# Retention block of a decoder trunk: the sample queries stand in pairs, at every second sample

## What is computed

```python
    def step(s, inp):
        qc, kc, vc = inp
        a = jnp.einsum('bnhk,bmhk->bhnm', qc, kc) * decay
        o = (jnp.einsum('bhnm,bmhv->bnhv', a, vc)
             + jnp.einsum('bnhk,bhkv->bnhv', qc, s) * xi[None, :, :, None])
        s = g_c[None, :, None, None] * s + jnp.einsum('bmhk,bmhv->bhkv', kc * zeta[None, :, :, None], vc)
        return s, o
...
    o, s = retention_scan(q, k, v, s0)
    mu = jnp.mean(o, axis=-1, keepdims=True)
    var = jnp.mean(jnp.square(o - mu), axis=-1, keepdims=True)
    o = (o - mu) * lax.rsqrt(var + GN_EPS)
    o = o.reshape(B, L, hv) * jax.nn.silu(g.astype(jnp.float32))
    return o.astype(xn.dtype) @ w_out, s
```

## Time and profile before

| | |
|---|---|
| time, median of 3 runs | 1866.96 us (1866.75 to 1867.14) |
| the profiled execution | 1866.61 us, span 1864.6 us |
| PE | 1791.1 us busy, 96% of the span |
| DVE, ACT, POOL | 52%, 47%, 46% |
| chain that ended last | PE 84%, DVE 6%, ACT 3%, DMA 3%, POOL 2% |
| DMA | 346.36 MB, mean 186 GB/s |

### The profile page before, as it was taken

The page is one execution under the profiler, slowest core; times in us unless marked ns, Lnnn a source line. Parts: engine busy times, 40 slices in busy tenths (PEclk is TensorE's granted clock), DMA queues, the critical chain, the costliest instruction groups (busy, mean ns, idle before and its releaser), DMA issues.

```text
span 1864.6 us, 33101 instructions
## 1 busy us (share of the span) xinstructions
PE 1791.1 (96%) x14552; PEld 1694.6 (91%) x14552; DVE 962.8 (52%) x1035; ACT 877.5 (47%) x1020; POOL 861.3 (46%) x246
## 2 busy tenths in 40 slices
PE   8999999999979999899999988999999999999998
PEld 7888888999969999898989878999998888889998
DVE  4444446675386753334344455776354444377743
ACT  4455545443454444444454445443454555544443
POOL 4554545545215554564444402355355544555551
PEclk9999999999989999999999979999999999999999
DMA  8767864555434556755555532455667778545552
GB/s 273 243 235 274 290 216 157 181 181 165 130 106 158 178 178 201 209 178 167 154 154 166 148 90 91 141 178 162 206 199 277 242 258 283 193 140 178 180 186 86
DMA packets 306037, 346.36 MB, mean 186 GB/s; under 512 B 7847, under 2 KB 269479, under 8 KB 305887
## 3 DMA queue, kind: packets, MB, share of 16 engines
q1 hardware_dynamic: 257968, 260.36, 44.3%
q10 hardware_dynamic: 47927, 83.90, 13.0%
HBM read 299.66 MB, written 44.82 MB: 185 GB/s over the span
## 4 chain that ended last, share of the span: by engine, by line
PE 84%; DVE 6%; ACT 3%; DMA 3%; POOL 2%; issue 1%; ACTq 1%; DVEq 0%; PEldq 0%
PE acc L1481 21%; PE acc L1488 20%; PE acc L1482 20%; PE mix L1889 2%; POOL w_lo L1385 2%; PE mix L1862 1%; PE mix L1543 1%; PE acc L1509 1%; DMA st<-in_state_ret_dram 1%; PE mix L1623 1%; PE acc L1510 1%; PE acc L1515 1%; PE mix L1642 1%; ACT w_hi L434 1%; PE mix L1612 1%
## 5 line engine op out<-in xcount | busy, mean ns | idle before, releaser
L1385 POOL TENSOR_TENSOR w_lo<-raw,w_hi 128x2048 fp32r<-128x2048 f32 (+2 forms) x181 | 777.4, 4302 | 596.8 <-ACT w_hi L434 596.8
L1481 PE MATMUL acc<-g_hi,w_hi 128*128 128x264 f32 x2544 | 640.9, 290 | 9.5 <-ACT w_hi L434 3.3
L1482 PE MATMUL acc<-g_lo,w_hi 128*128 128x264 f32 x2544 | 629.7, 285 | 0.0
L434 ACT ACTIVATE w_hi<-raw 128x2048 fp32r<-128x2048 f32 (+3 forms) x260 | 455.9, 1755 | 184.1 <-PE acc L1488 87.1
L1481 PEld LDWEIGHTS acc<-g_hi,w_hi 128*128 128x128 f32 x2544 | 480.1, 189 | 22.1 <-issue 16.4
L1482 PEld LDWEIGHTS acc<-g_lo,w_hi 128*128 128x128 f32 x2544 | 482.7, 190 | 1.3
L933 DVE TENSOR_TENSOR w_lo<-raw,w_hi 128x2048 fp32r<-128x2048 f32 (+2 forms) x79 | 334.2, 4231 | 238.7 <-ACT w_hi L434 238.7
L1488 PE MATMUL acc<-g_hi,w_lo 128*128 128x264 f32 x2544 | 342.1, 285 | 0.0
L1488 PEld LDWEIGHTS acc<-g_hi,w_lo 128*128 128x128 f32 x2544 | 325.3, 188 | 2.4 <-issue 1.3
L1419 POOL TENSOR_TENSOR h_lo<-hid,h_hi 128x528 fp32r<-128x528 f32 x44 | 59.0, 1340 | 330.3 <-ACT h_hi L707 330.3
L1481 PE MATMUL acc<-h_hi,w_hi 128*128 128x264 f32 x664 | 164.0, 284 | 0.0
(11 more groups left out here) (253 smaller groups left out, 2303.4 us busy)
## 6 DMA issues: line engine op xcount, KB each, us to landing
raw<-in_w_ffn_in_dram SPq DMA_DIRECT2D x88, 1024.0 KB, 5.2
raw<-in_w_in_ret_dram SPq DMA_DIRECT2D x48, 1024.0 KB, 7.4
raw<-in_w_in_attn_dram SPq DMA_DIRECT2D x36, 1024.0 KB, 5.4
st<-in_state_ret_dram ACTq DMA_DIRECT2D x64, 512.0 KB, 6.7
out_dram<-st ACTq DMA_DIRECT2D x64, 512.0 KB, 6.9
raw<-in_w_ffn_out_dram SPq DMA_DIRECT2D x32, 768.0 KB, 4.6
raw<-in_w_ffn_out_dram SPq DMA_DIRECT2D x32, 640.0 KB, 4.7
raw<-in_w_out_ret_dram SPq DMA_DIRECT2D x16, 1024.0 KB, 7.9
```

The source lines that it names most:

```text
L434: A(w_hi[:, u % SPL, 0:size[u]], raw[:, u % RAW, 0:size[u]], ACT.Copy).then_inc(hi_split, 1)
L1385: TT(w_lo[:, u % SPL, 0:size[u]], raw[:, u % RAW, 0:size[u]], w_hi[:, u % SPL, 0:size[u]].bitcast(F32), ALU.subtract).then_inc(lo_by_pool, 1)
L1481: MM(out, wh, x_hi[:, ks[k], :], start=first and k == 0, stop=False)
L1482: MM(out, wh, x_lo[:, ks[k], :], start=False, stop=False)
```

## The change

The queries of two samples stand directly behind each other, and the slots of the even samples hold the spread alone. Queries 0 and 1 stand ahead of the spread of sample 3, queries 2 and 3 ahead of that of sample 5, 4 and 5 ahead of that of sample 7, and 6 and 7 in slot 0 of the fifth unit. In the output stage the pairs follow the same rule, and the last two stand in one slot. Nothing else is changed; ACT, DVE, POOL and SP have the same instructions in the same order.

```diff
+                def queries(n):
+                    query(n)
+                    query(n + 1)
+
...
                 def sample(n):
-                    if n % 8 >= 2:
-                        query(n - 2)
+                    if n % 8 >= 3 and n % 2:
+                        queries(n - 3)
                     spread(n)
...
                         elif h and s == 4:
-                            samples = (lambda: query(8 * h - 1), lambda: turn_samples(gh - 1))
+                            samples = (lambda: queries(8 * h - 2), lambda: turn_samples(gh - 1))
...
                             ins.then_inc(tk_done, 1)
-                            if h:
-                                query(n)
...
                 proj(uo + 3, po + 1, ro_hi, ro_lo, pieces[0], first=False, last=False, done=0,
-                     between=(lambda: query(30), None, lambda: query(31)))
+                     between=(None, None, lambda: queries(30)))
```

## The result

The changed kernel takes 1875.26 us (median of 6 runs, 1871.30 to 1876.73) against 1866.89 beside it: ratio 1.0049, 95% interval 1.0037 to 1.0062. It is slower by 8.4 us where 6.0 was forecast. The profiled execution took 1873.08, span 1871.3.

The account below looks back on a forecast made before the run. PE, busy 96%, and the chain of states were taken to end each head block nearly together. Six blocks at 1.5 us late less 3.0 slack gave +6.0 on 1866.96, so 1873.0 us; range 1863.5 to 1880.

Parts of the forecast that it names:

- State 9's lateness: In each of six head blocks, state 9 would be scaled late on ACT; taken as 1.5 us per block.
- The first pair of bounds: State 9 late by 0.93 (query 4 moved) to 1.55 us (store of state 4 later), if transfers take as before.
- The bound by bytes: Load of state 5 and store of state 2 pushed into the full DMA stretch, 1.4 us each, 2.8 together.
- The load of state 7: On ACT in the block shown, issued behind the moved query 2 at 141.54 instead of 138.71, 2.83 us late.
- POOL's part ... covered too: In the head blocks, POOL's 4.3 us behind the later weight rounding would still be ready for the unit needing it.
- The slack: Spare time of o_rows before PE's turn: none in the first block, 0.81 second, 0.49 last, 3.0 us over six.
- The output stage: No gain from PE's saving there; load of state 6 up to 2.0 us late, counted as 0 for each layer.
- The sign named for this stage: PE's wait before the spread of sample 7 in the output stage longer by up to 1 us, its end unmoved.
- Absorbed: Rival: transfers absorb the lateness in the six blocks, 0.93 us or less each, giving 1867 to 1870; chance 0.24.
- Faster: Rival: states get past the weights, so each block's turn takes the whole 1.28 us, about 1859; chance 0.12.
- More bytes: Rival: 2.8 us of lateness per block plus 1.5 from the output stages, about 1882; chance 0.14.
- That pairing saves nothing on PE: Rival: the second query in a slot costs the full 0.76 us, giving 1875 to 1877; no chance of its own.

Follow-up runs that it names:

- st6_after: The changed kernel with six state buffers instead of five, room made by rq in one buffer and grstd in another tile; 1857.68 us, ratio 0.9956.
- late9: The changed kernel with ACT's scaling of state 9 moved from ahead of the sample rows to behind them; 1863.00 us, ratio 0.9982.
- ks_after: The changed kernel with k_s made from PSUM and the reciprocal instead of copied out of rk; 1883.02 us, ratio 1.0089 to the changed kernel.
- late9_ks: The changed kernel with state 9 scaled behind the sample rows and k_s made from PSUM; 1858.64 us, ratio 0.9953.
- out_only: The kernel before with the paired queries in the output stage alone, samples 24 to 31 of both layers; 1862.66 us, ratio 0.9985.
- ks_before: The kernel before with k_s made from PSUM and the reciprocal instead of copied out of rk; 1866.41 us, ratio 0.9996.
- round_first: The changed kernel with weight rounding and the even sample's store ahead of the waiting load on ACT, first four units; 1886.98 us, ratio 1.0103.
- round_only: The changed kernel with only the weight rounding put ahead of the waiting load on ACT; 1880.89 us, ratio 1.0071.

## Why the prediction was right, and where its steps were off

The direction, the place and the likeliest case were right: PE saves its 1.28 a block, the load behind the moved query goes out late, state 9 with it, and `o_rows` hands that to PE in all six blocks. The sum was 2.4 short: the blocks were put 5.3 too low, the output stages 2.5 too high, and 0.4 lie between the traces and the medians.

**State 9's lateness**, "I take 1.5 per block", was mis-sized: 0.73, 2.39, 2.76, 1.64, 3.26 and 3.15, mean 2.3. So the blocks cost 11.3, not 6.0; st6_after and late9 show that it is this lateness and its place ahead of `o_rows`, and nothing in the pairs, that costs it. The first pair of bounds, 0.93 to 1.55, failed: the store of state 4 went out 2.35 late in head 2 and the load of state 9 2.59. The bound by bytes, 2.8, came nearer. It named a load and a store pushed into the full stretch; what the trace shows is the stretch that they left empty, in the earlier trace rows the one with a share of 0.62: 0.85 MB, 2.2 us. That the full share means "that bytes count" was read rightly and then weighed too low. By the prediction's own sum the measured latenesses give 13.9 - 3.0 = 10.9 and a time of 1877.9, outside the 1870.7 to 1877 of its likeliest case. The gain of the output stages, which it had not counted, brought the time back: that part of the hit is luck.

**The load of state 7** was put at 141.54 in its block, 17.75 behind the first spread. In the first block of each layer it goes out at 17.77. In the other four it goes out at 18.5 to 18.8, 3.6 to 3.9 late instead of 2.83, since it then waits for the store of state 2 to land: the bracket at 144.21 names that store, which ACT issued 1.9 later than before, behind the late rounding (10.80 in the block instead of 8.91).

**"POOL's part ... covered too"** failed. Cover was judged by the unit that needs the weights, and the neighbour on DVE was overlooked. The updates of sample 4 came 2.0 to 2.4 us late, and PE's waits for updates rose from 3.9 us in 4 places to 9.6 in 16. In the changed kernel this cost nothing at the end (ks_after), because PE met the later wait at the turn anyway; with that one gone it cost 4.4 us (late9_ks against late9).

**The slack**, "3.0 over all six", was of the right size: the six latenesses add up to 13.9, and the blocks grew by 11.3, so 2.6.

**The output stage, "I count 0",** failed by a slip: the load of state 6 was said to go out up to 2.0 late with the moved query, but it waits for query 1, an odd one, which did not move. With PE earlier it went out earlier (11.11 instead of 11.80 in its stage), and the stage gained 1.0 and 1.5 (out_only: 2.9 in the medians). The sign named for this stage did not come either: the wait in front of the spread of sample 7 is 0.40, and was 0.64. The gain hid half of the error in the blocks.

**The rivals.** Absorbed: no, from 17 on the transfers of head 2 ran as full as before, and only 0.2 MB were made up ahead of that. Faster: the Trainium skill's TensorEngine Tiling (Array Packing), Key Properties, says that a change of tiling mode drains TensorE. The trace agrees that each visit costs PE time: st6_after gets 1.19 of the 1.28 per block, once the turn waits for PE alone. More bytes: its 2.8 a block was too much, at a mean of 2.3. That pairing saves nothing on PE is refuted by the slots.

## What to carry to other kernels

When a consumer is moved later on the engine that bounds, look first at who waits for its buffer: here an in-order queue that also holds roundings and stores stood behind that wait. Ask what the transfers move in the time of the wait; ahead of a full stretch, bytes not moved come back as lateness. Here 0.85 to 0.88 MB, 2.2 us at the rate of that stretch, stood against 2.4 to 3.3 us in four blocks. And a fix that gains nothing alone may be the one that counts when the wait behind it is gone, so the two are tried together, and each without the change as well.

## What the runs showed of the hardware that was not expected

A 128x16 copy from SBUF to SBUF on DVE took 0.17 us with POOL idle, 1.23 beside the tail of POOL's subtraction and up to 4.60 beside the whole of it, and then ended 0.02 to 0.04 behind it each time. The same values made from PSUM took 0.17 in all eight heads of ks_after, but there POOL was idle at that moment. ks_before settles it: in six of its heads POOL was in the middle of a subtraction, and they took 0.17 as well. One of them, in its timelines of DVE and POOL:

```profile
137.00 0.17 DVE L1085 TENSOR_TENSOR k_s<-acc,rstd_pre 128x16 f32<-128x16 f32 x1
...
134.31 4.63 POOL L1384 TENSOR_TENSOR w_lo<-raw,w_hi 128x2048 fp32r<-128x2048 f32 x1
```

The Trainium skill has the rule (SBUF — State Buffer, Who interferes with whom): a copy of DVE in its two-port mode and GpSimd take turns at a shared pair of ports, and the later one waits for the whole instruction of the other. The trace agrees in that the copy, which started later, ended with POOL each time; that it runs in that mode no row names. The first head of the kernel before had a like case in `q_xi`, which has both inputs in SBUF and took 4.11 beside POOL; it was there to be read.

The granted clock fell to near half behind some of PE's waits at the turn, as shown above. Three kernels that were to be no slower than after were slower by it, in part at least: ks_after, round_first and round_only.
